# Modulation pairs moved from attention to the short convolution

## The reference, cut to what matters

```
s_lat = silu(c)
for layer in range(2):
    mod = split(s_lat @ mod_w[layer] + mod_b[layer], 6)      # mod_w[layer]: 1024 x 6144
    h = modulate(rms_norm(x, norm_mix_pre), mod[0], mod[1])
    if layer == 0:   # deltanet and attention share one projection in and one out
        y = concat(deltanet(h @ w_in), attention(h @ w_in)) @ w_out
    else:            # short convolution
        gate_b, gate_c, xt = split(h @ w_in, 3)
        y = (gate_b * dwconv(gate_c * xt, conv_w)) @ w_out
    x = x + mod[2] * rms_norm(y, norm_mix_post)
    h = modulate(rms_norm(x, norm_ffn_pre), mod[3], mod[4])
    x = x + mod[5] * rms_norm(conv_ffn(h), norm_ffn_post)
```

## Time and profile before

| | us |
|---|---|
| median of 3 runs | 1708.76 |
| lowest, highest | 1706.11, 1711.48 |
| the profiled execution | 1714.39 |
| its span, first to last instruction | 1712.6 |
| TensorE busy in the span | 1576.1 |
| VectorE busy | 873.1 |
| ScalarE busy | 668.5 |
| GpSimd busy | 369.5 |
| mean granted TensorE clock, share of 2.4 GHz | 0.943 |

### The profile page before, as it was taken

The page is one execution under the profiler, slowest core; times in us unless marked ns, Lnnn a source line. Parts: engine busy times, 40 slices in busy tenths (PEclk is TensorE's granted clock), DMA queues, the critical chain, the costliest instruction groups (busy, mean ns, idle before and its releaser), DMA issues.

```text
span 1712.6 us, 19828 instructions
## 1 busy us (share of the span) xinstructions
PE 1576.1 (92%) x7752; PEld 1290.8 (75%) x7752; DVE 873.1 (51%) x1150; ACT 668.5 (39%) x1044; POOL 369.5 (22%) x255
## 2 busy tenths in 40 slices
PE   8899896669978886999999999989999999999997
PEld 2688786568965554868888888868888788888886
DVE  2654424887626676574444434464446644444222
ACT  2444536313436896224333332232233433343221
POOL 3028502346764663300000001100003000000000
PEclk9899898789985998989999999999998999999999
DMA  8325610001133453213333222213222233232231
GB/s 337 99 86 172 172 50 13 1 1 50 50 113 109 148 172 77 71 50 99 98 98 98 95 90 92 95 47 111 92 92 74 74 99 98 98 98 92 83 96 50
DMA packets 153907, 160.18 MB, mean 94 GB/s; under 512 B 11383, under 2 KB 151144, under 8 KB 152808
## 3 DMA queue, kind: packets, MB, share of 16 engines
q1 hardware_dynamic: 153344, 158.95, 28.9%
q10 hardware_dynamic: 488, 0.18, 0.0%
HBM read 157.03 MB, written 2.10 MB: 93 GB/s over the span
## 4 chain that ended last, share of the span: by engine, by line
PE 77%; DVE 10%; ACT 6%; POOL 3%; issue 2%; DMA 1%; SPq 0%; DVEq 0%; ACTq 0%; POOLq 0%
PE ps L502 19%; PE ps L503 19%; PE ps L504 19%; ACT mod_raw_c L1234 2%; DVE blocks_inv L1746 2%; DVE sub_prod L1743 1%; PE ps L557 1%; POOL mod_raw_c L2144 1%; PE ps L954 1%; PE ps L956 1%; PE ps L955 1%; PE ps L726 1%; PE ps L911 1%; DVE w_lo L1534 1%; PE ps L615 1%
## 5 line engine op out<-in xcount | busy, mean ns | idle before, releaser
L1534 DVE TENSOR_TENSOR w_lo<-w_raw,w_hi 128x2048 fp32r<-128x2048 f32 x100 | 232.1, 2321 | 495.3 <-ACT w_hi L1180 495.3
L502 PE MATMUL ps<-h_hi,w_hi 128*128 128x512 f32 x968 | 380.0, 393 | 2.0 <-DVE w_lo L1534 2.0
L503 PE MATMUL ps<-h_lo,w_hi 128*128 128x512 f32 x968 | 379.5, 392 | 0.0
L504 PE MATMUL ps<-h_hi,w_lo 128*128 128x512 f32 x968 | 378.9, 391 | 0.0
L1180 ACT ACTIVATE w_hi<-w_raw 128x2048 fp32r<-128x2048 f32 x100 | 191.3, 1913 | 317.6 <-PE ps L504 272.3
L502 PEld LDWEIGHTS ps<-h_hi,w_hi 128*128 128x128 f32 x968 | 183.3, 189 | 40.5 <-DVE w_lo L1534 2.5
L504 PEld LDWEIGHTS ps<-h_hi,w_lo 128*128 128x128 f32 x968 | 183.4, 189 | 38.7
L503 PEld LDWEIGHTS ps<-h_lo,w_hi 128*128 128x128 f32 x968 | 183.2, 189 | 37.8
L2257 POOL TENSOR_TENSOR sum_acc_y<-sum_acc_y,sum_y 128x512 f32<-128x512 f32 x18 | 27.0, 1502 | 588.8 <-ACT sum_y L1418 588.8
L2144 POOL TENSOR_TENSOR mod_raw_c<-mod_raw_c 128x1024 f32<-128x1024 f32 (+2 forms) x84 | 127.2, 1515 | 70.2 <-ACT mod_raw_c L1234 65.7
L502 PE MATMUL ps<-mid_hi,w_hi 128*128 128x512 f32 x338 | 132.9, 393 | 0.0
(11 more groups left out here) (347 smaller groups left out, 2688.5 us busy)
## 6 DMA issues: line engine op xcount, KB each, us to landing
w_raw<-in_ffn_w_up SPq DMA_DIRECT2D x44, 1024.0 KB, 5.1
mod_raw_c<-in_mod_w SPq DMA_DIRECT2D x28, 1024.0 KB, 5.4
w_raw<-in_ffn_w_down SPq DMA_DIRECT2D x16, 896.0 KB, 4.8
mod_raw_e<-in_mod_w SPq DMA_DIRECT2D x12, 1024.0 KB, 5.2
w_raw<-in_sc_w_in SPq DMA_DIRECT2D x12, 1024.0 KB, 5.2
w_raw<-in_hyb_w_in SPq DMA_DIRECT2D x9, 1024.0 KB, 7.7
mod_raw_a<-in_mod_w SPq DMA_DIRECT2D x8, 1024.0 KB, 16.2
w_raw<-in_ffn_w_down SPq DMA_DIRECT2D x8, 1024.0 KB, 5.1
```

The source lines that it names most:

```text
L502: mm(dst, hi, xh[:, k0 + k, :], start=first and k == 0, stop=False)
L503: mm(dst, hi, xl[:, k0 + k, :], start=False, stop=False)
L504: i = mm(dst, lo, xh[:, k0 + k, :], start=False, stop=last and k == nk - 1)
L1534: V.tensor_tensor(wlo[s][:, :], raw[s][:, :], f32(whi[s][:, :]), ALU.subtract).then_inc(sem("w_lo"), 1)
```

## The change

Attention's loop keeps pairs 20 to 27, one in every fourth block. Pairs 28 to 39 (`LATE` is 28) are loaded and worked off in the short convolution: pair 28+t goes with tile t of the gate projection (t from 0 to 7) and of the output projection (t from 8 to 11). ScalarE makes its products in tile t's turn, VectorE, not GpSimd, adds them in the turn of tile t+2, and TensorE takes its columns ahead of tile t+4. These pairs have five slots of their own, and their sums a ring of six. The first output unit of attention (12) is split in turn 16 of the loop, the second in turn 33, behind `turn_hi` of block 31. A part of the vectors is computed later (`later_weights`). Three semaphores are merged into others.

```diff
+        ATT0, LATE = EARLY + LEVEL_PAIRS, EARLY + LEVEL_PAIRS + 8
+        def mod_block(i, lag):
+            return [j for j in range(ATT0, LATE) if 4 * (j - ATT0) + lag == i]
         def slot_of(j):
-            return (j - EARLY) % 2 if j < EARLY + LEVEL_PAIRS else (0, 1, 3, 4, 5)[(j - EARLY - LEVEL_PAIRS) % 5]
+            return (j - EARLY) % 2 if j < ATT0 else (3, 5, 1)[(j - ATT0) % 3] if j < LATE else 1 + (j - LATE) % 5
+        def late_at(t):
+            return [j for j in range(LATE, PAIRS) if j - LATE == t]
+        def late_sums(j):
+            return 3 * (j - LATE + 1)
-        def mod_block(i, lag):
-            j0 = EARLY + LEVEL_PAIRS
-            return [j for j in range(j0, PAIRS) if 3 * (j - j0) // 2 + lag == i]
...
-            for j in range(EARLY, PAIRS):
+            for j in range(EARLY, ATT0 + 2):
                 load_mod_pair(j)
-            sp.wait_ge(sem("mod_done"), 2 * PAIRS)
+            sp.wait_ge(sem("mod_done"), 2 * ATT0 - 2)
             load_wout(12)
+            for j in range(ATT0 + 2, LATE):
+                load_mod_pair(j)
+            sp.wait_ge(sem("mod_done"), 2 * LATE - 4)
             load_wout(13)
...
+            for j in range(LATE, LATE + 5):
+                load_mod_pair(j)
             sqb(sc_in, U_SCIN + 8)
-            sqb(sc_out, U_SCOUT)
+            load_sc_out(U_SCOUT)
+            load_mod_pair(LATE + 5)
+            load_sc_out(U_SCOUT + 1)
+            load_mod_pair(LATE + 6)
+            load_mod_pair(LATE + 7)
+            load_sc_out(U_SCOUT + 2)
...
             def mod_columns(pairs):
                 for j in pairs:
-                    pe.wait_ge(sem("mod_acc"), acc_c(j))
+                    if j < LATE:
+                        pe.wait_ge(sem("mod_acc"), acc_c(j))
+                    else:
+                        pe.wait_ge(sem("late"), late_sums(j))
...
@@ tensor, out_units
+                        if j:
+                            for t in range(2):
+                                mod_columns(late_at(KC + t - 4))
                         continue
                     for r in range(2):
                         t = 2 * u + r
+                        if j:
+                            mod_columns(late_at(KC + t - 4))
@@ tensor, gate_b
                     for r in range(2):
+                        t = 4 * i + 2 * s + r
+                        if t == 4:
+                            pe.wait_ge(sem("scc"), KC)
+                            pe.wait_ge(sem("scu"), KC)
+                        mod_columns(late_at(t - 4))
                         pe.wait_ge(sem("scb"), cnt(4 * i + (2 * s + r - 3)))
@@ scalar, attention's loop
-                if i == A_HEADS * NQ:
-                    act.wait_ge(sem("mod_done"), 2 * PAIRS)
+                if i == 16:
                     split_hi(U_WOUT, 0)
+                if i == A_HEADS * NQ + 1:
+                    act.wait_ge(sem("mod_done"), 2 * LATE)
                     split_hi(U_WOUT + 1, 1)
@@ scalar, y_units
                     if u < 3:
                         split_hi(u0 + u + 2, u % 2)
+                    if j:
+                        for t in (2 * u, 2 * u + 1):
+                            late_products(KC + t)
@@ scalar, gate_b
+                    for r in range(2):
+                        late_products(4 * i + 2 * s + r)
@@ vector
+            def late_adds(j):
+                t, n = slot_tile(j), late_sums(j) - 3
+                dve.wait_ge(sem("mod_prod"), j - EARLY // 2 + 1)
+                V.tensor_tensor(t[:, 0:4, :], t[:, 0:4, :], t[:, 4:8, :], ALU.add).then_inc(sem("late"), 1)
+                dve.wait_ge(sem("late"), n + 1)
+                V.tensor_tensor(t[:, 0:2, :], t[:, 0:2, :], t[:, 2:4, :], ALU.add).then_inc(sem("late"), 1)
+                dve.wait_ge(sem("late"), n + 2)
+                if j >= LATE + 6:
+                    dve.wait_ge(sem("mod_done"), 2 * (j - 5))
+                V.tensor_tensor(lsum[:, (j - LATE) % 6, :], t[:, 0, :], t[:, 1, :], ALU.add).then_inc(sem("late"), 1)
@@ vector, y_units
-                        y_tile(j, 2 * u + r)
-                    if u < 3:
-                        split_lo(u0 + u + 2, u % 2)
+                        t = 2 * u + r
+                        y_tile(j, t)
+                        if j == 2 and t == KC - 2:
+                            later_weights()
+                        if r and u < 3:
+                            split_lo(u0 + u + 2, u % 2)
+                        if j:
+                            late_sums_at(KC + t - 2)
@@ vector, gate_b, behind the two low parts
+                    for r in range(2):
+                        late_sums_at(4 * i + 2 * s + r - 2)
```

More of the change, by code:

```diff
@@ L120, in hybrid_trunk @@
                   for i, a0 in enumerate((tmp_at, R + 73 * K))]
+        mraw_l = [view(region(f"mod_raw_l{i}", KC * UW, 40 + 8 * i), "p (k n) -> p k n", n=UW) for i in range(1, 6)]
+        lsum = view(region("late_sums", 6 * UW, 120), "p (j n) -> p j n", n=UW)
         macc = view(region("mod_sums", 6 * UW, 81), "p (j n) -> p j n", n=UW)
@@ L383, in load_mod_pair @@
                 s, users = slot_of(j), slot_users(j)
-                if users:
+                if users and users[-1] >= LATE:
+                    sp.wait_ge(sem("late"), late_sums(users[-1]))
+                elif users:
                     sp.wait_ge(sem("mod_done"), 2 * (users[-1] + 1))
-                elif s in (3, 4):
+                elif s == 3:
                     sp.wait_ge(sem("Z"), 4 * NT)
@@ L390, in load_mod_pair @@
                     sp.wait_ge(sem("S"), 2 * NT - 2)
-                sp.dma_start(mraw_c[s][:, :, :], mod_source(j)).then_inc(sem(f"mod_in{s}"), 16)
+                if j == LATE:
+                    sp.wait_ge(sem("tile"), 2 * U_SCIN)
+                sp.dma_start(slot_tile(j)[:, :, :], mod_source(j)).then_inc(sem(f"mod_in{s}"), 16)
             def raw_free(u):
@@ L518, in mm3_first, with mod_column @@
                             i.then_inc(sem(names[r]), 1)
-            def mod_column(m, acc):
-                mm(bank(7, 1, 16 + m), acc, ones[:, 0:1], start=True, stop=True).then_inc(sem("mod_done"), 1)
+            def mod_column(b, m, acc):
+                mm(bank(b, 1, 16 + m), acc, ones[:, 0:1], start=True, stop=True).then_inc(sem("mod_done"), 1)
             def mod_columns(pairs):
                 for j in pairs:
-                    pe.wait_ge(sem("mod_acc"), acc_c(j))
-                    acc = macc[:, j % 6, :] if j < EARLY else mraw_c[slot_of(j)][:, 0, :]
+                    if j < LATE:
+                        pe.wait_ge(sem("mod_acc"), acc_c(j))
+                    else:
+                        pe.wait_ge(sem("late"), late_sums(j))
+                    acc = macc[:, j % 6, :] if j < EARLY else slot_tile(j)[:, 0, :] if j < LATE else lsum[:, (j - LATE) % 6, :]
                     for part in range(2):
-                        mod_column(16 + 2 * j + part, acc[:, part * P:(part + 1) * P])
+                        mod_column(column_bank(j), 16 + 2 * j + part, acc[:, part * P:(part + 1) * P])
             def sum_columns(sq, idx, n, first, last):
@@ L1420, in y_squares, with late_products @@
                 nc.scalar.activation((qz[t % 2] if t else acc_z)[:, :], y[:, t, :], ACT.Square).then_inc(sem("zsq"), 1)
+            def late_products(t):
+                for jj in late_at(t):
+                    act.wait_ge(sem(f"mod_in{slot_of(jj)}"), landed(jj))
+                    products(slot_tile(jj))
             def y_units(u0, j):
@@ L1882, in _, with vec_part, post_weights @@
                         decayed_keys(k + 2 + d)
+            def vec_part(l, m, n, b):
+                V.tensor_tensor(modv[:, l, m:m + n, 0], bank(b, n, 16 + MODS * l + m), vec[:, 1, MODS * l + m:MODS * l + m + n],
+                                ALU.add).then_inc(sem("modv"), 1)
+            def post_weights(k, l, m, row):
+                return V.tensor_tensor(post_w[:, k, :], modv[:, l, m * KC:(m + 1) * KC, 0], vec[:, 0, row:row + KC], ALU.mult)
+            late_m = 2 * (LATE - MODS // 2 + 8)
             def norm_weights():
[L1884 to L1886 removed]
+                dve.wait_ge(sem("mod_done"), 2 * LATE)
+                vec_part(0, 16, MODS - 16, 7)
+                vec_part(1, 0, late_m, 7)
                 dve.wait_ge(sem("modv"), 3)
@@ L1889, in norm_weights, with later_weights, late_sums_at @@
                 pre_weights(2, 1, KC, 0, V_MIXPRE + KC)
-                pre_weights(3, 1, 4 * KC, 0, V_FFNPRE + KC)
-                for k, l, m, row in ((0, 0, 2, V_MIXPOST), (1, 0, 5, V_FFNPOST), (2, 1, 2, V_MIXPOST + KC), (3, 1, 5, V_FFNPOST + KC)):
-                    i = V.tensor_tensor(post_w[:, k, :], modv[:, l, m * KC:(m + 1) * KC, 0], vec[:, 0, row:row + KC], ALU.mult)
-                i.then_inc(sem("norm_w"), 1)
+                post_weights(0, 0, 2, V_MIXPOST)
+                post_weights(1, 0, 5, V_FFNPOST)
+                post_weights(2, 1, 2, V_MIXPOST + KC).then_inc(sem("norm_w"), 1)
+            def later_weights():
```

(12 more changed lines are left out.)

39 lines of the change are left out of this document (25 added, 14 removed).

## The result

The changed kernel takes 1746.78 us (median, 1744.54 to 1748.93) against 1710.12 for the kernel before on the same chip: 2.04% slower, ratio 1.0204 with an interval of 1.0177 to 1.0231. The forecast was 1739 in a range of 1712 to 1762. The profiled execution took 1748.3 us, its span 1746.5 against 1712.6, so 33.9 more.

The account below looks back on a forecast made before the run. ScalarE was taken as nearly full in attention's loop, TensorE in the gate projection. Attention -21, gate projection 22.9 + 5 and output projection 20.1 + 3 gave +30 us on the 1708.76 median: 1739, range 1712 to 1762.

Parts of the forecast that it names:

- The gate projection: Short convolution: TensorE waits 11.5 and 9.7 us for VectorE's sums, columns 1.7, together 22.9, plus 5 for the low clock.
- The output projection: Short convolution's later stage: tiles wait for VectorE's sums, two tiles take 16.1 us, loss 20.1 us, plus 3 for clock.
- The 3 us more for the clock: Output projection: 3 us more for low clock behind one wait of 4.4 us and five of about 2.
- the half speed behind the 1753: Output projection: if GpSimd sharing SBUF interfaces halved the speed of all moved VectorE adds, 14 us more, 1753.
- The tail: Behind attention's loop: last head's values start at 675 instead of 685, 10 us less, plus 1 for the clock.
- The loop: Attention's loop: 15 us less from fewer pairs, bounds 0 and 36; the split moved into block 16 costs 5.
- 23 x 0.49 = 11 us: Attention's loop: gain over the 23 distances from block 8 to block 31, 0.49 us each, 11 us.
- The period of 15.4: Attention's loop: four blocks with one pair take 15.4 us against 17.4 before, including TensorE's wait of 1.5.
- ScalarE is the loop's only bound: Rival, attention's loop: blocks without a pair all take 2.83 us, -6 us overall, 1703; chance 0.09.
- Only the gate's waits count: Rival: ScalarE and VectorE keep up in the output projection; +12 us, 1721; chance 0.18.
- The clock stays low in the output tiles: Rival, output projection: matmuls at 0.43 us bind the tiles, 19 us more, 1758; chance 0.18.
- The tail keeps its wait: Rival, behind attention's loop: the second split stays late, so the wait remains; +10 us, 1749; chance 0.02.

Follow-up runs that it names:

- Experiment 6: Changed kernel with TensorE taking all twelve late pairs' columns ahead of output tile 7, products and sums left in place; ratio 1.0076 to the kernel before.
- experiment 8: Changed kernel with the late pairs' sums on GpSimd instead of VectorE, products, loads and columns left in place; ratio 1.0173 to the kernel before.
- experiment 7: Changed kernel with both weight splits behind attention's loop again, at turn 32 and behind the wait for the columns; ratio 1.0197 to the kernel before.
- experiments 2 to 5: Changed kernel with attention's eight pairs two turns later (1.0124), one turn later (1.0183), or six (1.0231) or two (1.0183) unused matmuls in turns without values.
- Experiments 9 to 11: Changed kernel with late products spread, sums on GpSimd, columns bunched (0.9968); then also attention's pairs two turns later (0.9896); then also first split behind the loop (0.9844).
- experiment 9: Changed kernel with late products spread over ScalarE's units 50 to 61, sums on GpSimd, columns bunched, loads interleaved; ratio 0.9968 to the kernel before.
- experiment 1: Changed kernel with the twelve late pairs left out altogether, their loads too; ratio 0.9922 to the kernel before.

## Why the prediction was right, and where it was wrong

The time rose by 37 us where 30 were forecast, and came out 8 us above the 1739 (the forecast started from 1708.76). The costs behind attention were right in mechanism and size; attention's gain was half of the one forecast.

**The gate projection: right in mechanism and size.** The stage and what stands ahead of it take 26.5 us more; 27.9 were forecast. Waits of 11.5 and 9.7 ahead of tiles 4 and 6 were forecast, 10.92 and 9.41 are there, released by VectorE's sums as said; the adds, estimated at 1.2, 0.7 and 0.4, take 1.22, 0.69 and 0.42. Behind each wait nine matmuls run 0.43 us apart (the first from 1243.94 on), 2 us each time where 2.5 were taken. Experiment 6, which moved only the columns, removed both waits; in experiment 8, which took the sums out of VectorE's turn, 3.3 us of them are left.

**The output projection: right, but for the clock.** Tile 2 was to start 17.9 us behind the stage's start and tile 7 58.2; they did so at 18.2 and 59.0. Two tiles were to take 16.1 us and take 16.0 (1299.51 to 1315.53) and 17.1 (to 1332.61), with VectorE idle for 2.41 us behind the squares, as said (2.1). This step rests on the trace of the changed kernel; no run moved the products alone. The 3 us more for the clock did not show: the stage costs 20.4, not 23.1. Behind the wait ahead of tile 2 and the one ahead of tile 6, matmuls 0.43 us apart for the most part filled time in which TensorE would have waited for VectorE anyway: the sums for tile 7 end at 1340.23, and TensorE takes their columns at 1340.29. So tiles 3 and 7 had no wait, and of the five waits of about 2 us that were to show the mechanism, ahead of tiles 3 to 7, only those of 0.78, 1.86 and 2.84 are there.

**GpSimd beside VectorE.** The Trainium skill (GPSIMD Engine Reference, Key points) states that GpSimd contends with VectorE instructions that have two SBUF inputs. It gives no size there; the half speed behind the 1753 was the prediction's own "if". The trace agrees in direction: of the moved adds in the output projection only single ones stretch (0.69 to 1.64, 0.42 to 1.37). The rows bear out neither a doubling nor a full immunity.

**The tail: right size, half of the reason.** 10 and 1 were forecast, 9.7 measured. But the working names the two splits as what stands ahead, and experiment 7 shows that 6.3 of it comes without moving a split; by the releasers it is the weights' load. They said so in the trace of before, and the prediction didn't follow them. The clock wasn't kept up by the shorter wait: matmuls run at 1.2 GHz until 678.

**The loop: wrong, and this is the step that failed.** The first eight blocks gained 6.5 (4 forecast). The split cost 6.3 (5). But "23 x 0.49 = 11 us" for the other distances came to 1: these 23 take 105.4 us instead of 99.9, with 6.3 of split in them. The period of 15.4 counted the wait of 1.5 and then TensorE's rows at full clock. Three quarters of the miss are the clock behind that wait: 15.8 with filler, 17.06 without. The prediction charged the clock for waits in every other stage and not in the one where it comes back every four blocks. 1.66 us in each of 5.75 periods is 9.5, nearly the whole of the 10 that this term missed. It is more than the 8 us by which the time came out above the forecast; the costs behind attention, 4 us too high, made up for a part.

**The rivals.** "ScalarE is the loop's only bound" falls with the period of 17.1. "Only the gate's waits count" falls with tile 7 at 59.0. "The clock stays low in the output tiles" falls: it is 0.88 and 0.93 over 1300 to 1350 us. "The tail keeps its wait" falls with 2.71.

What stays open: experiments 2 to 5 take 626 to 627 us from boundary to boundary, against 623.9 in the changed kernel, with the same code there. Experiments 9 to 11, whose code is the same there too, differ by 4 us among themselves, so this may be scatter. How much of the 48 us the sums' engine, the products' place and the columns' place cost singly is not shown either, beyond the gate's waits.

## What to carry to other kernels

When work moves to a stage with idle engines, ask not whether an engine has room but behind which instruction the work stands there and who waits for its last product: twelve pairs cost about 48 us in one order and 5 to 8 in another (experiment 9: 5 from boundary to boundary against the kernel before, 8 by the ratios against experiment 1). Follow a wait to the releaser in brackets before naming its cause. And price a short wait in a loop of short matmuls twice, once for itself and once for the matmuls at the lower clock behind it.

## What the hardware showed unexpectedly

Behind a wait of 1.56 us in each period of the loop TensorE fell to 1.2 GHz: the six value matmuls that follow stand 0.43 us apart instead of 0.23, and the loss (1.24 us) is nearly that of the wait. Useless matmuls of 1.56 us in its place brought the clock over these stretches from 0.91 and 0.88 to 0.99 and 1.00 and made the loop 6.7 us shorter, though the gain of the whole kernel is within the noise of the ratios. With the wait divided in two, of 0.63 and 1.06 us, the clock was 0.96 and 0.92. On GpSimd, adds of 1024 and 512 columns took 2.4 and 1.3 us where VectorE takes 1.22 and 0.69.
